# The first layer's 16 modulation blocks as matrix products on TensorE, and x loaded and squared in eight pieces

## The reference

```python
c_act = jax.nn.silu(c)
c_ctx_act = jax.nn.silu(c_ctx)
for layer in range(DEPTH):
    mod_l = jnp.split((c_act @ ada_w[layer] + ada_b[layer])[:, None, :], N_MOD, axis=-1)
    mod_c = jnp.split(c_ctx_act @ ada_w[layer] + ada_b[layer], N_MOD, axis=-1)
    h_l = modulate(rms_norm(x_l, norm_pre_mix[layer]), mod_l[0], mod_l[1])
    h_c = modulate(rms_norm(x_c, norm_pre_mix[layer]), mod_c[0], mod_c[1])
    o_c, o_l = token_mixing(h_c, h_l, w_in[layer], w_out[layer], ...)
    ...
```

## Time and profile before

| | |
|---|---|
| median of three runs | 4887.69 us (4882.37 to 4888.0) |
| the profiled execution | 4880.41 us, span of its instructions 4878.6 us |
| TensorE busy | 3894.2 us, 80% of the span |
| VectorE busy | 2166.4 us, 44% |
| ScalarE busy | 1409.2 us, 29% |
| GpSimd busy | 1153.4 us, 24% |

### The profile page before, as it was taken

The page is one execution under the profiler, slowest core; times in us unless marked ns, Lnnn a source line. Parts: engine busy times, 40 slices in busy tenths (PEclk is TensorE's granted clock), DMA queues, the critical chain, the costliest instruction groups (busy, mean ns, idle before and its releaser), DMA issues. The chain is left out here.

```text
span 4878.6 us, 81882 instructions
## 1 busy us (share of the span) xinstructions
PE 3894.2 (80%) x33358; PEld 3146.5 (64%) x33358; DVE 2166.4 (44%) x2979; ACT 1409.2 (29%) x1927; POOL 1153.4 (24%) x884
## 2 busy tenths in 40 slices
PE   1999539685868899999992999549658868999995
PEld 0888425363757788888881787425437757888884
DVE  6444734465545523232235323735465545332234
ACT  3111433234333421221213211433243334222221
POOL 0000520202531232232321000520205512333332
PEclk7999769796988999999996999669779988999997
DMA  3444110101012111111101234110110022111112
GB/s 133 157 163 166 50 59 0 38 1 36 5 35 83 65 35 36 39 35 40 35 31 60 103 125 148 41 48 1 38 35 4 4 73 79 48 43 52 47 47 86
DMA packets 69839, 283.38 MB, mean 58 GB/s; under 512 B 7072, under 2 KB 12448, under 8 KB 64928
## 3 DMA queue, kind: packets, MB, share of 16 engines
q1 hardware_dynamic: 53696, 199.03, 12.1%
q10 hardware_dynamic: 15840, 79.96, 4.5%
HBM read 223.65 MB, written 47.45 MB: 56 GB/s over the span
## 5 line engine op out<-in xcount | busy, mean ns | idle before, releaser
L3422 DVE SCALAR_TENSOR_TENSOR y<-ps,taps,y 128x1023 f32<-128x1023 f32 (+1 forms) x132 | 134.1, 1016 | 865.2 <-DVEq L3420 858.7
L453 PE MATMUL ps<-h_hi,wu_hi 128*128 128x512 f32 x1680 | 460.5, 372 | 12.2 <-PEq L3322 12.2
L453 PE MATMUL ps<-h_hi,wu_raw_rest 128*128 128x512 f32 x1680 | 459.4, 371 | 0.0
L453 PE MATMUL ps<-h_whole_rest,wu_hi 128*128 128x512 f32 x1680 | 459.3, 371 | 0.0
L3467 POOL TENSOR_TENSOR wu_raw_rest<-wu_raw,wu_hi 128x1024 fp32r<-128x1024 f32 x84 | 201.3, 2397 | 1032.1 <-POOLq L3466 1032.1
L453 PE MATMUL ps<-h_hi,w_hi 128*128 128x512 f32 (+1 forms) x1200 | 313.9, 366 | 86.2 <-PEq L449 86.0
L453 PEld LDWEIGHTS ps<-h_hi,wu_hi 128*128 128x128 f32 x1680 | 294.6, 188 | 69.6 <-issue 13.7
L453 PEld LDWEIGHTS ps<-h_hi,wu_raw_rest 128*128 128x128 f32 x1680 | 294.5, 188 | 56.5
L453 PEld LDWEIGHTS ps<-h_whole_rest,wu_hi 128*128 128x128 f32 x1680 | 294.6, 188 | 56.2
L453 PE MATMUL ps<-h_hi,w_raw_rest 128*128 128x512 f32 (+1 forms) x1200 | 312.1, 364 | 0.0
L453 PE MATMUL ps<-h_whole_rest,w_hi 128*128 128x512 f32 (+1 forms) x1200 | 312.0, 364 | 0.0
(11 more groups left out here) (377 smaller groups left out, 8209.5 us busy)
## 6 DMA issues: line engine op xcount, KB each, us to landing
wu_raw<-in_w_up_dram SPq DMA_DIRECT2D x88, 512.0 KB, 3.3
w_raw<-in_w_in_dram SPq DMA_DIRECT2D x54, 512.0 KB, 4.7
ada_w<-in_ada_rest_dram ACTq DMA_DIRECT2D x27, 1024.0 KB, 7.2
rows<-rows ACTq DMA_DIRECT2D x42, 640.0 KB, 6.2
wd_raw<-in_w_down_dram SPq DMA_DIRECT2D x40, 512.0 KB, 4.2
raw<-rows SPq DMA_DIRECT2D x24, 640.0 KB, 4.0
ada_w<-in_ada_rest_dram ACTq DMA_DIRECT2D x27, 512.0 KB, 5.0
h_whole<-rows SPq DMA_DIRECT2D x20, 640.0 KB, 5.7
```

Of the source, the lines that this page charges most:

```text
L453: mm = pe.matmul(ps[:, lo:lo + width], w[a][:, t, :], rhs[b][:, t, lo:lo + width], start=(t == 0 and i == 0), stop=(t == n_k - 1 and i == 2))
L3422: dve.scalar_tensor_tensor(y[:, s, lo + 1:hi], ps[s][:, lo:hi - 1], k.taps[:, s, 0:1], y[:, s, lo + 1:hi], ALU.mult, ALU.add).then_inc(own ...
```

## The change

In layer 0 the 16 blocks become products on PE. `ada_w`'s first 2048 columns are stored as they are (rows of 1024 inputs on the partitions, in 8 pieces i of 128 x 2048, 1 MB each). For each piece, four float32 products with the two vectors as the stationary operand (`cond`, 128 x 2) and 512 columns of the piece as the moving one add up in four banks of PSUM, as 2 rows of 2048. ACT copies the rows to SBUF, PE turns them in 16 transposes, and DVE adds `ada_b` in one instruction in place of the 32 products, their 32 read-outs and 4 additions. The even pieces come on SP's DMA queue, the odd ones on ACT's. PE does pieces 0 to 3, then the sum over partitions (now L451), then pieces 4 to 7.

`xT` is loaded in eight pieces, one semaphore each, and `load_phase` no longer waits for it; ACT waits for a piece before it squares it. The two vectors come a second time in columns (`cond_cols`, 128 x 16) and have a Silu of their own. `cact` is loaded behind the first weights and, in layer 0, once the transposes are done; its Silu now stands behind `norm.scalar` on ACT, in both layers.

```diff
                 sp.dma_start(k.ada_b[:, :], a["ada_b"]).then_inc(x_in, 16)
-                sp.dma_start(k.xT[:, :, :], a["xT"]).then_inc(x_in, 16)
+                sp.dma_start(k.cond[:, :, :], a["cond_cols"]).then_inc(x_in, 16)
+                for t in range(KD):
+                    sp.dma_start(k.xT[:, t, :], a["xT"][:, t, :]).then_inc(k.x_tiles[t].sem, 16)
                 sp.wait_ge(x_in, 48)
...
-        self.ada_in = k.sems(st, "ada_in", 4)
         self.own_a, self.own_v, self.own_p = (k.sem(st, s) for s in ("norm_act", "norm_dve", "norm_pool"))
-
-    def load_ada(self, eng, quarters):
-
-        for i in quarters:
-            place, first, n = self.ada_parts[i]
-            eng.dma_start(place, self.ada[:, first:first + n]).then_inc(self.ada_in[i], 16)
+        self.ada_in = [k.mark(f"ada_in{i}") for i in range(KD)]
+        self.cond_done, self.ada_done, self.rows_done, self.turned = (
+            k.mark(s) for s in ("ada_cond", "ada_done", "ada_rows", "ada_turned"))
+
+    def load_ada(self, eng, first):
+
+        for i in range(first, KD, 2):
+            eng.dma_start(self.ada_place(i), self.ada[:, i]).then_inc(self.ada_in[i].sem, 16)
...
+            self.load_ada(sp, 0)
...
-            self.load_ada(act, (1, 3))
+            self.load_ada(act, 1)
+            act.activation(k.cond[:, :, :], k.cond[:, :, :], ACT.Silu).then_inc(self.cond_done.sem, 1)
         for t in range(KD):
+            if self.ada is not None:
+                act.wait_ge(k.x_tiles[t].sem, k.x_tiles[t].at(16))
...
         act.sem_inc(self.root_dve, 1)
+        if self.ada is not None:
+            act.wait_ge(self.ada_done.sem, self.ada_done.at(1))
+            for i, place in enumerate(self.ada_sums):
+                ins = act.activation(self.ada_rows[:, i, :], place, ACT.Copy)
+            ins.then_inc(self.rows_done.sem, 1)
...
-            dve.wait_ge(self.cond_dve, 1)
-            dve.sem_inc(self.cond_dve, -1)
-            for i in (0, 2, 1, 3):
-                dve.wait_ge(self.ada_in[i], 16)
-                dve.sem_inc(self.ada_in[i], -16)
-                place, first, blocks = self.ada_parts[i]
-                modulation_blocks(dve, k, place, first, blocks, own)
+            dve.wait_ge(self.turned.sem, self.turned.at(1))
+            dve.tensor_tensor(k.all_mods[:, 0:N_FIRST, :], self.ada_turned[:, 0:2 * N_FIRST].rearrange("p (n s) -> p n s", s=2),
+                              widen(k.ada_b[:, 0:N_FIRST], 2), ALU.add).then_inc(own, 1)
+            dve.wait_ge(own, 1)
+            dve.sem_inc(own, -1)
             combine_gain(dve, k, 0, 1, own)
...
     def tensor(self, pe):
+        if self.ada is not None:
+            self.ada_products(pe, 0, KD // 2)
         pe.wait_ge(self.acc_pe, 1)
         pe.sem_inc(self.acc_pe, -1)
         for lo, w in SEGS:
@@ -433,7 +451,24 @@
                 mm = pe.matmul(self.ps[:, lo:lo + w], self.k.const(C_ONES), self.acc[:, lo:lo + w],
                                start=True, stop=True)
         mm.then_inc(self.sum_act, 1)
-
+        if self.ada is not None:
+            self.ada_products(pe, KD // 2, KD)
+            pe.wait_ge(self.rows_done.sem, self.rows_done.at(1))
+            for i in range(N_FIRST):
+                row = self.ada_rows[:, i // 4, i % 4 * P:(i % 4 + 1) * P]
+                mm = pe.transpose(self.ada_turned[:, 2 * i:2 * i + 2], row, self.k.const(C_IDENT)[0:2, 0:2])
+            mm.then_inc(self.turned.sem, 1)
+
+    def ada_products(self, pe, first, last):
+        if first == 0:
+            pe.wait_ge(self.cond_done.sem, self.cond_done.at(1))
+        for i in range(first, last):
+            pe.wait_ge(self.ada_in[i].sem, self.ada_in[i].at(16))
+            for c, place in enumerate(self.ada_sums):
+                mm = pe.matmul(place, self.k.cond[:, i, :], self.ada_place(i)[:, c * 512:(c + 1) * 512],
+                               start=(i == 0), stop=(i == KD - 1))
+        if last == KD:
+            mm.then_inc(self.ada_done.sem, 1)
...
-            early = k.h[:, :, :].rearrange("p t n -> p (t n)").rearrange("p (n c) -> p n c", c=D_MODEL)
-            late = ada_w[:, :, :, :].rearrange("p s n c -> p (s n) c")
-            spare = k.mix[:, 0:2 * D_MODEL].rearrange("p (n c) -> p n c", c=D_MODEL)
-            norm.ada_parts = [(early[:, 0:5], 0, 5), (early[:, 5:10], 5, 5), (late, 10, 4),
-                              (spare, 14, 2)]
-        norm.cond_dve = cond_dve
+            early = k.h[:, :, :].rearrange("p t n -> p (t n)").rearrange("p (i c) -> p i c", c=2 * D_MODEL)
+            late = ada_w[:, :, :, :].rearrange("p s n c -> p s (n c)")
+            extra = k.banks(st, "ada_sums", 2)
+            norm.ada_place = lambda i: early[:, i] if i < 5 else late[:, i - 5] if i < 7 else k.mix[:, 0:2 * D_MODEL]
+            norm.ada_sums = [ps[0][0:2, 512 * c:512 * c + 512] for c in range(3)] + [extra[0:2, 0:512]]
+            norm.ada_turned = extra[:, 512:1024]
+            norm.ada_rows = k.cact[0:2, :, :].rearrange("p s (i c) -> p (s i) c", c=512)
...
-                sp.dma_start(k.cact[:, :, :], a["cond"]).then_inc(cond_in, 16)
                 norm.sync(sp)
                 load(sp, 0, N_IN - 1)
                 load(sp, 1, 0)
+                if layer == 0:
+                    sp.wait_ge(norm.turned.sem, norm.turned.at(1))
+                sp.dma_start(k.cact[:, :, :], a["cond"]).then_inc(cond_in, 16)
...
+                norm.scalar(act, lambda: [round_weights(act, s) for s in range(2)])
                 act.wait_ge(cond_in, 16)
                 act.sem_inc(cond_in, -16)
                 act.activation(k.cact[:, :, :], k.cact[:, :, :], ACT.Silu).then_inc(own_a, 1)
                 act.wait_ge(own_a, 1)
                 act.sem_inc(own_a, -1)
                 act.sem_inc(cond_dve, 1)
-                norm.scalar(act, lambda: [round_weights(act, s) for s in range(2)])
                 load_item(act, 0, first_tile)
...
-    out["ada_first"] = ada[:N_FIRST].transpose(1, 0, 2)
+    out["ada_first"] = np.asarray(ada_w)[0][:, :N_FIRST * P].reshape(KD, P, N_FIRST * P).transpose(1, 0, 2)
+    out["cond_cols"] = np.stack([np.asarray(c)[0], np.asarray(c_ctx)], 1).reshape(KD, P, 2).transpose(1, 0, 2)
```

More of the change, by code:

```diff
@@ L313, in __init__, with close @@
         self.even_pe, self.odd_pe, self.spilled = k.sem(st, "even_pe"), k.sem(st, "odd_pe"), k.sem(st, "spilled")
-        self.ada_in = k.sems(st, "ada_in", 4)
         self.own_a, self.own_v, self.own_p = (k.sem(st, s) for s in ("norm_act", "norm_dve", "norm_pool"))
-    def load_ada(self, eng, quarters):
-        for i in quarters:
-            place, first, n = self.ada_parts[i]
-            eng.dma_start(place, self.ada[:, first:first + n]).then_inc(self.ada_in[i], 16)
+        self.ada_in = [k.mark(f"ada_in{i}") for i in range(KD)]
[4 more added lines that the diff above has]
+            eng.dma_start(self.ada_place(i), self.ada[:, i]).then_inc(self.ada_in[i].sem, 16)
+    def close(self):
+        if self.ada is not None:
+            for m in self.ada_in + self.k.x_tiles:
+                m.base += 16
+            for m in (self.cond_done, self.ada_done, self.rows_done, self.turned):
+                m.base += 1
     def sync(self, sp):
         if self.ada is not None:
-            self.load_ada(sp, (0, 2))
+            self.load_ada(sp, 0)
         if self.spill is not None:
@@ L582, in _ @@
                     dve.sem_inc(ada_free[s], 1)
-                if layer:
-                    dve.wait_ge(cond_dve, 1)
-                    dve.sem_inc(cond_dve, -1)
+                dve.wait_ge(cond_dve, 1)
+                dve.sem_inc(cond_dve, -1)
                 rest_of_weights(dve, 0)
@@ L632, in _ @@
                     act.sem_inc(out_free[s], -16)
+        norm.close()
 def residual_phase(k, y, x, n, m_gate, reload=None):
@@ L3759, in build @@
         k.eps = k.sb(st, "eps", [P, 1])
-        k.dots = k.sb(st, "dots", [P, 5, 2])
+        k.dots = k.sb(st, "dots", [P, 2, 2])
+        k.cond = k.sb(st, "cond_cols", [P, KD, 2])
+        k.x_tiles = [Mark(k.sem(st, f"x_tile{t}")) for t in range(KD)]
         k.all_lb = k.sb(st, "lb", [P, DEPTH, 8])
```

## The result

The changed kernel takes 4855.08 us (median of four runs, 4849.34 to 4857.53), the kernel before beside it 4886.33 (4882.37 to 4888.0). The ratio is 0.9937, 95% interval 0.9924 to 0.9949: **31 us, 0.63%, faster**, where the prediction said 4857.0 and 30.7 less. The profiled execution of the changed kernel took 4849.34, its span 4847.2.

The account below looks back on a forecast made before the run. DVE's products held layer 0's scaling 42 us behind the factor; 8.2 us before layer 1's squares were also on the path. Gains 22.5 + 8.2 = 30.7 took 4880.4 to 4849.7, plus 7.3 for the median: 4857.0; range 4843 to 4880.

Parts of the forecast that it names:

- Who sets the start: Layer 0, first use of the gain: DVE's products set its start at 94.57, 42 us behind ACT's factor at 52.5.
- When the pieces are there: Layer 0 loads: piece 0 lands at 30.5 us behind x, pieces 2, 4, 6 follow at 2.5 us each.
- The removed wait: Layer 0, squares no longer wait for x and `cact` (27.63 to perhaps 12): costs and brings nothing, covered by PE's products.
- The products: Layer 0 on PE: 64 instructions at 0.43 us after a slow start of about 4.3 us, the last product at 62.6.
- Behind them: Layer 0 after the products: copies 2.6 us, transposes 2.5, then 1.08 + 3.16 as now; scaling at 72.1, gain 22.5.
- Layer 1: Start of layer 1: squares no longer wait for `cact`, a table load and Silu; gains 8.2 us.
- The Silu: Large Silu behind the norm: its 3.5 us cost nothing, covered by ACT's 4.76 us wait for the first tile.
- DVE's wait as long as now: Sign in the changed kernel's profile: DVE's wait for the weights behind the norm stays as long as before.
- All slow: Rival, layer 0: all products stay at 1.2 GHz, 0.86 us each; scaling at 101.1, total time 4886 us; chance 0.13.
- half slow: Rival, layer 0: half of the products go at 1.2 GHz; total time about 4871 us; chance 0.05.
- slower: Rival, layer 0: at 1.2 GHz weight loads add 0.34 us to each of 64 instructions, 21.8 more, 4908 us; chance 0.03.
- The fourth: Rival, layer 0: SP's queue served first, PE starts at 20.5, ends at 52.6; total time 4847 us; no chance of its own.

## Why the prediction was right

The mechanism was right in both layers. The time of the profiled execution was met more closely, 4849.34 us against 4849.7, than the terms were: by the rows the two layers gained 32.0 us instead of 30.7, and executions drift by more than that. So the last microsecond of the agreement is luck.

*Who sets the start.* DVE's products did, 42 us behind the factor; the row after shows the factor at 54.4, as predicted to the tenth, and the start at 70.61.

*When the pieces are there.* 30.5 predicted, 30.66 measured, but by two errors that cancel, and that is luck. The last byte of piece 0 came at about 29.9, not 28.9. I had counted 421 GB/s from 4 us on the earlier trace rows; the changed kernel's row for the same stretch ends in 391:

```profile
4.00:16.00 12.00, 0.00 (x0) 0.00 (x0) 2.26 (x2) 8.37 (x14) 0.00 (x0) 1.00 0.99 391
```

That is 0.36 MB less, or 0.9 us (SP's twelve issues, too, ended at 7.2, not 6.3). And behind the last byte lay 0.75 us, not the 1.6 that I had taken from the 4.8 us of the earlier trace rows. The course in between was another than I had drawn: ScalarE's queue issued at 8.54, moved nothing until 12.2 and then took its pieces at 254 GB/s (three in 12.4 us), near the 257 of the earlier trace rows, so that its last piece landed at 30.3 (issued at 10.05, landed 20.3 us later) and not at 25.3 + 1.6. For piece 0 this made no difference: in both courses x and all four odd pieces are through ahead of its last byte. The run with x waited for shows where it does: there SP's queue had no x ahead of piece 0, the late queue wasn't in my sum, and the start was off by 2.5 us.

*The removed wait.* "Costs and brings nothing itself" is the step that was wrong, without a bearing on the time forecast: putting the wait on x back brought the scaling 7.0 us forward.

*The products.* "I take the same pace" for 2 stationary columns as for 128 held: 0.85 and 0.43 us. The start was slow for 4.5 us, against 4.3, and the last product stood at 61.82, against 62. "PE was at 0.50 wherever it started anew" was too strong as a reading: at 42.98 in the kernel before, the granted clock reads 1.00 (from 42 to 46 us), though the loads stand 0.85 us apart, the slow pace. The rule that the prediction set against this (the Trainium skill, page "TensorE: Matmul & The Clock Gate", section "HAM oscillation — how this bites in real kernels") finds its case in none of these products, since once begun they never waited. It has something like it in the run with four column tiles: there PE waited 2.07, 2.08 and 3.06 us ahead of the second, third and fourth piece, the eight instructions of a piece went in two groups of four, 0.81 us apart, which is the pace of 1.2 GHz, and the sum behind them took 4.53 us instead of 2.42.

*Behind them.* These terms were too large: the copies took 2.0 us (2.6 predicted), the transposes 1.36 (2.5). The scaling stood at 70.61 instead of 72.1, and layer 0 gained 24.0 instead of 22.5. Sixteen transposes of two columns cost about what eight of 128 do (1.07 and 1.97 us in the earlier trace rows); their spread over the runs is 1.15 to 1.86 us. The lower end of my bracket for them, 1.9, should have been 2 x 1.07 = 2.1.

*Layer 1.* 8.2 predicted, 8.0 in the rows, 7 and 8 us in two experiments.

*The Silu.* "So I cost it at nothing" held, but the cover named was the wrong one. ScalarE's wait of 4.76 us shrank to 1.84 and is not what ends first. What ends first is the time until PE needs the weights of its third tile, whose load follows ScalarE's collecting of the first: that has 0.6 us left. "DVE's wait as long as now" was 12.90 and became 14.45 us.

*The rivals.* All slow, half slow and slower are refuted by the one row at 36.21: loads 0.43 us apart and within the product ahead. The fourth, more gain by an earlier start, didn't happen by itself, since the queues shared; two experiments made it happen and gave 7.0 and 12.7 us at the scaling, and with column tiles and the copies moved as well it was 20.7.

## What to carry to other kernels

When a product moves to PE, follow three things by rows: which piece it waits for first (the order of the products should be that of the landings), what stands in the next engine's stream ahead of the result's use, and only then its own length. A product made four times as fast gave 2 us; the same products begun 13 us sooner gave 12.7, and six lines of ScalarE's stream in another order gave 6. An operation that is moved into a wait is priced not by that wait but by the nearest successor that stands still if it comes later, and running it three times shows how much cover is left.

## What the runs showed of the hardware

- A float32 product with a stationary operand of 2 columns costs PE what one with 128 costs: 0.43 us for each of its two instructions of 512 columns, 0.85 at the slow pace. The pace rose from the one to the other 4.5 us after the first such product, as it did after some 4 us with 128 columns at 1154.
- Four float32 products in four column tiles run at once: 0.43 us for four instructions, one of each, instead of 1.72; the last 16 products took 3.6 us instead of 13.8.
- ScalarE's DMA queue moved its first packet 3.7 us after its first issue (8.54 to 12.2), 3.8 us with x waited for (19.07 to 22.9) and 3.4 us in the kernel before (26.70 to 30.13). Each time it was the queue's first transfer of the run, and SP's queue had megabytes ahead or beside it. Most of its later transfers began 1.0 to 1.6 us after their issue, also where SP's queue was moving weights; so a busy neighbour alone doesn't explain it. Which of the other two does, no run here shows.
- From the last byte of a 1 MB piece to the product that waited for it were about 0.75 us; from x's last packet (26.80) to the square that waited for it (27.60), 0.8.
- Behind a standstill of 3.3 us PE ran its first products at full pace and then fell to a granted clock of 0.50 for some 3 us (the run with three Silus).
